# Order of the first two projections, direct broadcast of the first modulation rows, and modulation summed once per attention stage

## The reference, cut to what matters

```
for layer in range(2):
    mod_l = split(silu(c) @ ada_w[layer] + ada_b[layer], 6)       # 6 rows of 1024
    mod_c = split(silu(c_ctx) @ ada_w[layer] + ada_b[layer], 6)
    p_l = modulate(rmsnorm(x, g), mod_l[0], mod_l[1]) @ w_in[layer]   # likewise p_c of the context
    ya = mla_mixer(q, ckv, kr ...)      # keys and values from rmsnorm(ckv) @ w_ukv, rotary keys kr
    yb = swa_mixer(q, k, v ...)         # sliding window
    yc = na_mixer(q, k, v ...)          # neighbourhood
    yd = retention_mixer(q, k, v, gates ...)
    x  = x + mod_l[2] * (concat(ya, yb, yc, yd) * mix_beta @ w_out)
    h2 = modulate(rmsnorm(x, g2), mod_l[3], mod_l[4])
    x  = x + mod_l[5] * peer_ffn(h2)    # top 16 of 128 x 128 keys in 8 heads, gathered u and v
return rmsnorm(x, final_g)
```

## Time and profile before

| | us |
|---|---|
| median of 3 runs (lowest, highest) | 4947.29 (4945.28, 4955.01) |
| the profiled execution | 4945.98 |
| its span | 4944.2 |
| TensorE busy | 3247.7 (66%) |
| VectorE busy | 3128.9 (63%) |
| ScalarE busy | 913.5 (18%) |
| GpSimd busy | 1495.9 (30%) |

### The profile page before, as it was taken

How to read it: one execution, slowest core, us unless ns; L and a number is a source line. 1 busy time by engine, 2 the same in 40 slices (tenths; PEclk the granted TensorE clock), 3 DMA queues, 4 the chain that set the end, 5 groups by cost and what they waited for, 6 DMA issues and landing times.

```text
span 4944.2 us, 48806 instructions
## 1 busy us (share of the span) xinstructions
PE 3247.7 (66%) x16212; PEld 1259.8 (25%) x16212; DVE 3128.9 (63%) x8329; ACT 913.5 (18%) x2479; POOL 1495.9 (30%) x1376
## 2 busy tenths in 40 slices
PE   5888899665787555455545558898887545555545
PEld 2345445331232111111111114655332111111111
DVE  1242323687877878778777861523378787877876
ACT  1242311111111111111111121421111111111211
POOL 0000000334343443444444430000034444444443
PEclk7889998787897777877787778898888787777777
DMA  4132321799999999999999971011299999999998
GB/s 150 62 120 86 124 69 64 306 414 410 408 418 415 403 416 405 418 417 404 418 415 404 412 299 45 1 34 39 87 416 390 416 411 414 404 418 414 401 420 342
DMA packets 290749, 1496.72 MB, mean 303 GB/s; under 512 B 25432, under 2 KB 83928, under 8 KB 126656
## 3 DMA queue, kind: packets, MB, share of 16 engines
q0 software_dynamic: 185888, 1347.13, 66.3%
q1 hardware_dynamic: 73680, 114.85, 6.9%
q10 hardware_dynamic: 30928, 31.61, 1.9%
HBM read 1482.91 MB, written 10.58 MB: 302 GB/s over the span
## 4 chain that ended last, share of the span: by engine, by line
DVE 39%; PE 30%; DMA 19%; issue 7%; ACT 4%; POOL 1%; DVEq 0%; ACTq 0%; POOLq 0%; SPq 0%
DMA X<-in_uv_dram,X 18%; DVE X L1599 16%; PE ps L458 9%; PE ps L852 5%; DVE X L1610 2%; PE ps L627 2%; PE ps L819 2%; PE ps L668 2%; ACT X L1217 2%; DVE X L1516 1%; DVE X L1518 1%; DVE X L1519 1%; DVE X L1606 1%; PE ps L639 1%; PE ps L706 1%
## 5 line engine op out<-in xcount | busy, mean ns | idle before, releaser
L852 PE MATMUL ps<-X 64*64 64x512 f32 x2560 | 1640.1, 774 | 1408.9 <-DVE X L1610 1404.7
L1720 POOL DMA_INDIRECT X<-in_uv_dram,X x1280 | 1420.5, 1110 | 2167.9 <-PE ps L855 1629.3
L1599 DVE CUSTOM_DVE_ANT_0 X<-yT,X 128x1024 f32<-128x1024 f32 x1280 | 1532.9, 1223 | 340.2 <-DMA X<-in_uv_dram,X 306.8
L853 PE MATMUL ps<-X 64*64 64x512 f32 x2560 | 1640.2, 774 | 0.0
L855 PE MATMUL ps<-X 64*64 64x512 f32 x2560 | 1640.2, 774 | 0.0
L854 PE MATMUL ps<-X 64*64 64x512 f32 x2560 | 1640.2, 774 | 0.0
L852 PEld LDWEIGHTS ps<-X 64*64 64x64 f32 x2560 | 360.1, 163 | 2621.2 <-DVE X L1610 1972.8
L1217 ACT ACTIVATE X<-X 128x1 f32<-128x1 f32 x1280 | 258.6, 203 | 2338.4 <-DVE X L1599 2315.7
L855 PEld LDWEIGHTS ps<-X 64*64 64x64 f32 x2560 | 360.4, 163 | 0.0
L854 PEld LDWEIGHTS ps<-X 64*64 64x64 f32 x2560 | 360.3, 163 | 0.0
L853 PEld LDWEIGHTS ps<-X 64*64 64x64 f32 x2560 | 360.2, 163 | 0.0
(11 more groups left out here) (245 smaller groups left out, 3438.4 us busy)
## 6 DMA issues: line engine op xcount, KB each, us to landing
wring<-in_ada_w_dram SPq DMA_DIRECT2D x48, 1024.0 KB, 5.4
wring<-in_w_in_dram SPq DMA_DIRECT2D x24, 1024.0 KB, 5.5
wring<-in_peer_wq_dram SPq DMA_DIRECT2D x24, 1024.0 KB, 25.6
X<-in_uv_dram,X POOLq DMA_INDIRECT x1280
wring<-in_w_out_dram SPq DMA_DIRECT2D x8, 1024.0 KB, 5.1
X<-scores ACTq DMA_DIRECT2D x64, 128.0 KB
X<-mods ACTq DMA_DIRECT2D x15, 512.0 KB, 8.6
yT<-mods ACTq DMA_DIRECT2D x8, 512.0 KB, 9.1
```

What stands on the lines that cost most here:

```text
L852: pe.matmul(ps[0:HD, h, :], dg(slice(0, HD), s), v0[0:HD], **ends)
L853: pe.matmul(ps[HD:P, 2 + h, :], dg(slice(HD, P), s), v0[HD:P], **ends)
L1599: v.tensor_tensor_reduce(uvr[:, slot, 0:D], h2[:, t, :], uvr[:, slot, 0:D], 1.0, 0.0, ALU.mult, ALU.add, adot[:, s_:s_ + 1]).then_inc(S("d ...
L1720: g.indirect_dma_start(uvr[:, slot, :], None, a["uv"], bass.IndirectOffsetOnAxis(ap=istages[i % 2][:, s:s + 1], axis=0)).then_inc(S(f"uv{s ...
```

## The change

It does this:

- Head of layer 0: the first four chunks are spread by matmuls straight into tables on all partitions: 128-column weights `pick_wide` and `ones_wide`, for each chunk two streams (context and latent) times two matmuls. ScalarE copies the shift tables (`head_shift`), VectorE adds one and multiplies the gain while it takes the scale tables out of PSUM. These four chunks are not written to DRAM and not read back.
- The second projection starts behind the first. Transposes of latent, queries and rotary keys stand between its halves. Its own transposes follow, then the keys and values of latent attention, then attention. The queries get a row buffer of their own for all six tiles (`qrow`).
- `rows_chunk` runs its second half tile by tile; `free` is a function of the tile.
- Late modulation: the weights are shifted in `cT` by two columns per chunk, so that all chunks of an attention stage add into the same bank, on different partitions. There are 8 chunks in the first attention (pairs 0, 1, 3, 4, 6, 7, 9, 10), 6 in each other one and none behind c5. Sum, bias, copy and write happen once per stage.

```diff
+MOD_PAIRS = {"mla": (0, 1, 3, 4, 6, 7, 9, 10), "swa": (0, 2, 4, 6, 8, 10), "na": (0, 2, 4, 6, 8, 10)}
+MOD_KINDS = {"mla": (0, MOD_FIRST, 8), "swa": (1, 0, 6), "na": (1, 6, 6)}
-                    after = {1: mod[0:12], 3: mod[12:18], 5: mod[18:]}
+                    after = {1: mod[0:14], 3: mod[14:20]}
@@ rows_chunk
+                    order = [(i, kk) for kk in range(GROUP_K) for i in range(len(tiles))]
+                    if half:
+                        order.sort()
+                    for i, kk in order:
@@ TensorE, head
+                    def spread(c):
+                        pe.wait_ge(S("mpc"), c + 1)
...
+                        for s in range(2):
+                            pe.matmul(ps[:, 2 * (c % 2) + s, :], pick_wide[:, s, :], mrow[:, c % 2, :], start=True, stop=False)
+                        pe.wait_ge(S(f"ab{c % 2}"), 16 * (c // 2 + 1))
+                        for s in range(2):
+                            m = pe.matmul(ps[:, 2 * (c % 2) + s, :], ones_wide[0:1, :], adab[0:1, c % 2, :], start=False, stop=True)
@@ TensorE, late modulation
+                    at = MOD_WIDE - 2 * i
                     for half in range(2):
                         g = take(1)
                         for j in range(GROUP_K):
+                            m = pe.matmul(ps[32 * j:32 * j + 32, 6, :], cT[:, half * GROUP_K + j, at:at + 32], wring[:, g % WRING, j, :],
+                                          start=(i == 0 and half == 0), stop=(i == len(MOD_PAIRS[kind]) - 1 and half == 1))
+                def late_sum(kind):
+                    b, n_ = MOD_ORDER.index(kind), len(MOD_PAIRS[kind])
+                    pe.wait_ge(S("bpc"), b + 1)
+                    pe.matmul(ps[0:2 * MOD_MOST, 6, :], picks, mod_late[0], start=True, stop=False)
+                    pe.wait_ge(S("bb"), 16 * (b + 1))
+                    pe.matmul(ps[0:2 * MOD_MOST, 6, :], bias_to[0:n_, :], mod_late[1][0:n_, :], start=False, stop=True).then_inc(S("bps"), 1)
@@ TensorE, projections
+                def turn_latent_and_queries():
+                    pe.wait_ge(S("ckn"), B("ckn", L) + TILES)
+                    for t in range(TILES):
+                        m = pe.transpose(ps[:, 6 + t // 4, (t % 4) * P:(t % 4 + 1) * P], ckv[:, t, :], ident[:, :])
+                    m.then_inc(S("ckt"), 1)
+                    pe.wait_ge(S("cke"), B("cke", L) + 1)
+                    for t in range(lo, TILES):
...
+                        for h in range(HEADS):
+                            m = pe.transpose(ps[0:MLA_QK, 6 + t % 2, h * P:(h + 1) * P],
+                                             qrow[:, t, h * MLA_QK:(h + 1) * MLA_QK], ident[:, :])
+                        m.then_inc(S("qt"), 1)
...
+                rows_chunk(L, range(TILES), S("c1"), turn_latent_and_queries, ctx_from=GW, free=c0_out)
@@ ScalarE, head
+                def head_shift(c):
+                    act.wait_ge(S("mps"), c + 1)
+                    for s in range(2):
+                        m = nc.scalar.activation(norm_tables[0][0][:, 2 * s + 1, c * CH:(c + 1) * CH], ps[:, 2 * (c % 2) + s, :], ACT.Copy)
+                    m.then_inc(S("mtab"), 1)
@@ TensorE, behind c5 and the state matmuls
-                if L < LAST:
-                    late_parts(*MOD_LAST[0])
...
-                    late_parts(*MOD_LAST[1])
-                    late_sum(*MOD_LAST[1])
```

More of the change, by code:

```diff
@@ L451, in rows_chunk @@
                     g = take(1)
[L452 to L461, removed]
+                    order = [(i, kk) for kk in range(GROUP_K) for i in range(len(tiles))]
+                    if half:
+                        order.sort()
+                    for i, kk in order:
+                        k, t = half * GROUP_K + kk, tiles[i]
+                        if k == 0 and free:
+                            free(t)
+                        c0 = ctx_from if L == LAST and t < CT else 0
+                        m = pe.matmul(ps[:, t, c0:CH], hT_or_y[0][:, k, t * P:(t + 1) * P],
+                                      wring[:, g % WRING, kk, c0:CH], start=(k == 0), stop=(k == KD - 1))
+                        if k == KD - 1 and t != tiles[-1]:
+                            m.then_inc(ready, 1)
                     if half == 0:
@@ L471, in _, with head_modulation @@
                 lo = first_out[L]
[L472 to L482, removed]
+                def head_modulation():
+                    def spread(c):
+                        pe.wait_ge(S("mpc"), c + 1)
+                        if c == 2:
+                            pe.wait_ge(S("mtab"), 1)
+                        if c == 3:
+                            pe.wait_ge(S("mtab"), 2)
+                        pe.wait_ge(S("picked"), 1)
+                        for s in range(2):
[3 more added lines that the diff above has]
+                            m = pe.matmul(ps[:, 2 * (c % 2) + s, :], ones_wide[0:1, :], adab[0:1, c % 2, :], start=False, stop=True)
+                        m.then_inc(S("mps"), 1)
+                    for c in range(MOD_FIRST):
                         if c >= 2:
-                            pe.wait_ge(S("mrow"), B("mrow", M) + c - 1)
+                            pe.wait_ge(S("mpc"), c - 1)
                         for half in range(2):
@@ L514, in _ @@
                     pe.wait_ge(S("silu"), 1)
-                    pe.wait_ge(S("picked"), 1)
-                    modulation(0, range(MOD_FIRST))
+                    head_modulation()
                     pe.wait_ge(S("in"), 16 * 7)
@@ L943, in squares, with load_tables @@
                         nc.scalar.activation(stat[:, 1, t:t + 1], stat[:, 0, t:t + 1], ACT.Sqrt, scale=1.0 / D, bias=eps[:, 0:1]).then_inc(S("n_rt"), 1)
-                def load_tables(M, tag, chunks):
-                    for q in range(2):
-                        act.wait_ge(S(f"ms{q}"), B(f"ms{q}", M) + 16 * (chunks // 2))
+                def load_tables(M, tag):
+                    act.wait_ge(S("bst"), 32 * (3 if M else 1))
                     tabs, gain = norm_tables[tag]
@@ L1032, in _ @@
                 sq_out(TILES - 1)
+                for h in range(HEADS):
+                    act.wait_ge(S("kn"), B("kn", L) + h + 1)
+                    b = 2 * (h % 2)
+                    nc.scalar.activation(km[0:HD, h, :], ps[0:HD, b:b + 2, :].rearrange("p a b -> p (a b)")[:, 0:TOK], ACT.Copy).then_inc(S("kne"), 1)
                 def attention(kind):
@@ L1198, in _ @@
                 if L < LAST:
[L1199 to L1200 removed]
+                    act.wait_ge(S("bst"), 32 * len(MOD_ORDER))
                 def load_gate(s):
@@ L1350, in _ @@
                     v.wait_ge(S("rop2"), B("rop2", L) + t - CT + 1)
+                for t in range(TILES):
+                    v.wait_ge(S("vmm"), B("vmm", L) + t + 1)
+                    v.tensor_copy(vm[:, t, :], ps[:, 4 + t % 2, 0:GW]).then_inc(S("vme"), 1)
                 def attention(kind):
```

278 lines of the change are left out of this document (126 added, 152 removed).

## The result

The changed kernel takes 4877.11 us (median of 4 runs, 4871.58 to 4880.18); the kernel before, on the same chip, 4947.55 (4945.28 to 4955.01). The ratio is 0.9854, with a 95% interval of 0.9842 to 0.9867: 70.4 us less, where 48.3 were forecast. The time lies 2.9 us under the low end of the range.

The account below looks back on a forecast made before the run. TensorE was taken to bound the mixing stages, with expert stages (VectorE, gathers) untouched. Terms summed to 48.3 us: 4945.98 - 48.3 + 1.3 = 4899 us, with an 8-in-10 range of 4880 to 4922.

Parts of the forecast that it names:

- Head, minus 10: Layer 0's head: modulation rows spread by matmuls without the DRAM trip start the norm earlier; minus 10 us.
- Second projection behind the first, minus 7.4 and 6, and attention's start, minus 2: Around the first two projections: reordering saves 7.4 us in layer 0, 6 in layer 1; attention starting partly fast saves 2.
- The second half then starts at the low clock for a while: Second projection's second half, after the transposes: a slow start costing 1 us in layer 0, 0.6 in layer 1.
- the 9.5 and 7.4 left open: Between the second projection's halves: transposes and copies take 9.5 us in layer 0, 7.4 in layer 1.
- without this cover: VectorE's rotary, squares and latent scalings: hidden beside the next half's 20.7 us; uncovered, they would cost what they do now.
- Modulation in attention: Layer 0's latent-query, window and neighbourhood attention: fewer modulation pieces save 5, 6 and 4.5 us.
- The price per sum: Layer 0's window and neighbourhood attention: each removed sum gives 1.2 and 0.9 us, part returning as lower clock.
- Behind the last projection: Layer 0, before the state matmuls: one part and one sum go, minus 3.75 us; the other chunk gives nothing.
- Tile by tile: Last output projections' second halves: less VectorE work remains at the end, minus 2.3 and 1.3 us, 3.6 together.
- ScalarE's copies at nothing: Attention: ScalarE loses 17 pairs of copies and their DMA issues, but waits there, so nothing is gained.
- Rival A: Window and neighbourhood attention, second projection, attention's start: the clock takes gains back; 4916 us, chance 0.22.
- Rival B: Head, middles of the second projections and window attention run fast: 13 us more gain, 4886 us; chance 0.15.

Follow-up runs that it names:

- e1: Changed kernel with the old head alone: first four modulation rows written to DRAM and read back as tables; 4886.78 us.
- e2: Changed kernel with the old order around the first two projections and a row buffer of three tiles, tile by tile kept; 4901.21 us.
- e7: Changed kernel with transposes of latent, queries and rotary keys ahead of the second projection instead of between its halves; 4890.77 us.
- e5: Changed kernel with the old modulation of the late chunks: part, sum, copies, bias load and write per chunk, at the old places; 4907.1 us.
- e9: Changed kernel with 14 added pieces of two unused matmuls in layer 1's window and neighbourhood attention; 4896.93 us.
- e3: Changed kernel with 13 pairs of zero-weight matmuls where layer 0's attention had its sums, without copies, DMAs or waits; 4891.05 us.
- e6: Changed kernel with 26 ScalarE copies put back in layer 0's attention stages, with no waits and results unread; 4876.14 us.
- e4: Changed kernel with second halves of all row projections in the old order instead of tile by tile; 4877.45 us.
- e11: e8 with one dummy matmul per pair in both layers' window attention, where TensorE waits for ScalarE's scaled rows; 4829.16 us.
- e10: e8 without the mixing: buffer of six tiles kept, then all window transposes, all keys, all values; 4859.52 us.
- e8: Changed kernel with a six-tile buffer for the second projection too, its transposes mixed with key and value matmuls; 4850.63 us.
- e12: e11 with more filler: one matmul per pair in layer 1's neighbourhood attention, nine behind each layer's state matmuls; 4823.13 us.

## Why the prediction was wrong

The mechanism and the direction were right; two terms were mis-sized, the modulation by 10.7 and the order by 8.7. The first is in part unexplained; the second is the clock and the row buffer.

- **Head, minus 10**: right (e1: 9.7). Single profiles show the fast and the slow course of the clock, 12.3 and 6.7 ahead of e1's c0, so a single one could have shown either.
- **Second projection behind the first, minus 7.4 and 6, and attention's start, minus 2**: a step that failed. e2 measured 24.1 for 15.4. It failed at "The second half then starts at the low clock for a while", and at the 9.5 and 7.4 left open, priced from transposes that stood between long waits. Behind a projection half, without those waits, they run at the high clock: 7.0 and 5.6. That VectorE's chain "without this cover" would "cost what they do now" was wrong too: uncovered it ends 3.9 us behind the projection (e7), since the new row buffer frees ScalarE and with it VectorE. Attention's start was meant for both layers at 1 each: layer 1's gained 4.1, by a high clock from its first us on, layer 0's nothing.
- **Modulation in attention, minus 5, 6 and 4.5**: 22.5 (7.4, 7.3, 7.8) instead of 15.5 in the profile of e5, above the forecast in all three and above the bound of 6 in the first. The price per sum, 1.2 and 0.9 in the second and third, rested on a comparison of two layers, which differ in more than the sums; the pieces in layer 1 cost 1.4 each (e9). But it isn't what e5's time convicts: by it 13 pieces cost 16, and e3 measured 14 (19.0 in the profiles' stages). The step that failed is that a sum was taken to cost its two matmuls and nothing else. Beyond the pieces e5 costs 16 more, where the forecast had 3.75, all of it behind the last projection. In the attentions and c2 the profiles show 5.7 of it, which is not ScalarE's copies alone, put at nothing (e6); TensorE's waits for them and the clock are left, not separated.
- **Behind the last projection, minus 3.75**: 4.1 in place, and the second chunk at nothing, both right. Not foreseen: 1.8 at the start of c4, and 1.4 behind the states, of which 1.1 is in the first half of the output projection.
- **Tile by tile, minus 3.6**: right at the place (2.7 and 1.7), not to be told in the time (e4).
- **ScalarE's copies at nothing, experts at nothing**: right (e6; 2118.7 against 2120.3, the last stage 3.7 shorter, within what the gathers vary).

Two slips in the working changed little: the low end of the open middle, 7.8, adds up to 8.4 from its own items, and 15 sums leave the attention stages, not 17, which are all 20 less the three that stay.

The four undone parts add up to 9.7 + 24.1 + 30.0 + 0.3 = 64.1 of 70.4; the remaining 6 may be the scatter of four medians or gains that need more than one part, and no run tells which.

Rival A (4916) missed by 39, but its mechanism is real in one stage. Neighbourhood attention of layer 0, changed kernel:

```profile
485.33:569.37 84.04, 70.49 (x420) 38.28 (x421) 39.57 (x114) 34.21 (x86) 11.27 (x16) 0.84 0.42 145
```

Without its sums it stood at 0.84, with them (e3) at 0.89, so part of them did come back as a lower clock. What outweighed it lay elsewhere: from c0 to the first score the clock rose from 0.91 to 0.95 in layer 0 and from 0.90 to 0.96 in layer 1, where the change takes waits away. Rival B (4886) named the right places and was 9 short. The trace had a hint. Window attention stood at 0.76 with TensorE waiting 12.7 us in all for ScalarE's scaled rows, 2.4 at most in one go; e11 filled such waits, and the clock rose.

The Trainium skill, page "TensorE: Matmul & The Clock Gate", section "HAM oscillation", on which rival A leaned, tells of bursts between waits for transfers that each start slow. Between the projections it spoke for the change, which takes waits away there, though for ScalarE and VectorE and not for transfers. e11 agrees that waits matter, at 2.4 us and less, and with ScalarE as the one waited for.

The Trainium skill, page "DMA: Bandwidth & Descriptors", section "Anatomy of one DMA", from which 3 us were put beside the head's 10, was used in one part only: its time of a transfer is the fixed part plus the bytes at 436 GB/s. Two fixed parts and the five loads of 512 KB come to an estimate of 4.0 + 6.0 = 10.0 us by that page, near the 10.9 from 57.78 to 68.74. The section is on transfers that GpSimd issues; these were ScalarE's, and no run here tells the two parts apart.

## What to carry to other kernels

Price an edit at both levels of the clock, and ask first whether it takes away waits between short TensorE instructions: such an edit can bring its own time and part of its neighbours' clock. Don't take the clock's answer from another stage; test it with a few dummy matmuls. A row buffer that holds all tiles of a stage lets ScalarE copy without waiting for transposes; for the second projection it gave 8.5 and 7.7 us in the two layers (e10).

## What the runs showed of the hardware

- The same instructions of window attention in layer 0 took 93.7 (e8), 97.0 (e7), 98.1 (e1), 99.2 (e2), 99.3 (e10), 99.7 (the changed kernel) and 101.3 us (e4, e9), at mean granted clocks of 0.82 down to 0.73. e9 and the changed kernel have all instructions up to there in common and differ by 1.6, so not all of this comes from what ran before. A difference of a few us in one profile's stage is no finding.
  The Trainium skill, page "TensorE: Matmul & The Clock Gate", section "Part 1: The HAM clock gate", says that the number of slow matmuls at a start varies from run to run. The head shows it: 2 slow matmuls in the changed kernel's profile, 8 in e8's, with the same instructions.
- Sixteen dummy matmuls in the waits for ScalarE's rows (2.4 us and less) saved 21.5 us; the granted clock rose from 0.69 to 0.91 in layer 1 and from 0.82 to 0.94 in layer 0.
- Filler doesn't always help: a wait of 10.8 us filled to 2.9 left the short matmuls behind it at 0.50, for 36 us in which TensorE had no gap (e12).
